# First query chunk interleaved with the input's transposes, small gates unit moved to the value chunks

## The reference, cut to what matters

```python
h = rms_norm(x, norm_g)
proj = jnp.einsum('bsd,dn->bsn', h, w_in)
(q_a, k_a, v_a, o_a, i_a, f_a, z_a, c_q, c_kv, k_r, z_b, g_a, g_b) = jnp.split(proj, offsets, axis=-1)
qk_a = jax.nn.silu(causal_depthwise_conv(jnp.concatenate([q_a, k_a], axis=-1), conv_w))
...
h_a = mlstm_chunkwise(q, k, v, i_a + gate_bias[:H_A], f_a + gate_bias[H_A:])
```

## Time and profile before

| | |
|---|---|
| median of 3 runs | 2112.98 us (2112.61 to 2113.32) |
| the profiled execution | 2112.74 us |
| its span, first to last instruction | 2110.7 us |
| TensorE busy | 2090.6 us, 99% |
| VectorE busy | 1446.0 us, 69% |
| ScalarE busy | 1088.2 us, 52% |
| mean granted clock of TensorE | 0.999 |

### The profile page before, as it was taken

How to read it: one execution, slowest core, us unless ns; L and a number is a source line. 1 busy time by engine, 2 the same in 40 slices (tenths; PEclk the granted TensorE clock), 3 DMA queues, 4 the chain that set the end, 5 groups by cost and what they waited for, 6 DMA issues and landing times.

```text
span 2110.7 us, 24975 instructions
## 1 busy us (share of the span) xinstructions
PE 2090.6 (99%) x10067; PEld 1754.5 (83%) x10067; DVE 1446.0 (69%) x1868; ACT 1088.2 (52%) x1409; POOL 39.2 (2%) x50
## 2 busy tenths in 40 slices
PE   8999999999999999999999999999999999999998
PEld 6888888888888888888888888888888888888886
DVE  5878788875555776556554455566896896797684
ACT  5545555555444675554445454354544554454453
POOL 0000000000000020000000000000000000000000
PEclk9999999999999999999999999999999999999999
DMA  7455555565465544365745542455555465556562
GB/s 270 181 182 197 200 186 213 182 243 193 172 218 198 189 147 171 125 235 199 294 179 181 191 167 100 160 200 185 196 204 193 168 231 185 185 189 219 182 218 98
DMA packets 56563, 402.60 MB, mean 191 GB/s; under 512 B 6240, under 2 KB 6496, under 8 KB 9216
## 3 DMA queue, kind: packets, MB, share of 16 engines
q1 hardware_dynamic: 53648, 380.67, 50.0%
q0 software_dynamic: 2656, 19.81, 2.4%
q10 hardware_dynamic: 144, 0.52, 0.1%
HBM read 392.59 MB, written 8.39 MB: 190 GB/s over the span
## 4 chain that ended last, share of the span: by engine, by line
PE 96%; ACT 1%; DVE 1%; issue 1%; DMA 0%; SPq 0%; POOLq 0%; POOL 0%; DVEq 0%; ACTq 0%
PE proj L617 15%; PE proj L619 15%; PE proj L618 15%; PE proj L1080 11%; PE proj L1083 6%; PE proj L722 4%; PE proj L723 4%; PE proj L724 4%; PE tbank L724 2%; PE tbank L723 2%; PE tbank L722 2%; PE tbank L576 2%; PE bank_a L722 1%; PE bank_a L724 1%; PE bank_a L723 1%; PE bank_b L724 1%
## 5 line engine op out<-in xcount | busy, mean ns | idle before, releaser
L1726 DVE TENSOR_TENSOR w_lo<-raw,w_hi 128x1024 fp32r<-128x1024 f32 x630 | 748.8, 1199 | 521.1 <-ACT w_hi L1186 513.9
L1186 ACT ACTIVATE w_hi<-raw 128x1024 fp32r<-128x1024 f32 x630 | 652.4, 1041 | 757.2 <-PE proj L619 480.8
L617 PE MATMUL proj<-w_hi,a_both 128*128 128x512 f32 x1280 | 513.3, 401 | 0.0
L619 PE MATMUL proj<-w_hi,a_both 128*128 128x512 f32 x1280 | 499.9, 391 | 0.0
L618 PE MATMUL proj<-w_lo,a_both 128*128 128x512 f32 x1280 | 498.4, 389 | 0.0
L619 PEld LDWEIGHTS proj<-w_hi,a_both 128*128 128x128 f32 x1280 | 240.2, 188 | 51.8
L618 PEld LDWEIGHTS proj<-w_lo,a_both 128*128 128x128 f32 x1280 | 240.7, 188 | 47.8
L617 PEld LDWEIGHTS proj<-w_hi,a_both 128*128 128x128 f32 x1280 | 240.6, 188 | 47.0
L1080 PE MATMUL proj<-a_both,w_hi 128*128 128x512 f32 x672 | 168.4, 392 | 0.3 <-DVE a_both L1772 0.3
L1080 PEld LDWEIGHTS proj<-a_both,w_hi 128*128 128x128 f32 x672 | 121.0, 189 | 22.2 <-DVE a_both L1772 0.5
L1186 ACT ACTIVATE w_hi_deep<-raw 128x1024 fp32r<-128x1024 f32 x84 | 85.7, 1025 | 94.1 <-PE proj L1083 57.6
(11 more groups left out here) (519 smaller groups left out, 3000.9 us busy)
## 6 DMA issues: line engine op xcount, KB each, us to landing
raw<-stream SPq DMA_DIRECT2D x359, 1024.0 KB, 4.8
nat<-x SPq DMA_DIRECT2D x4, 512.0 KB, 8.2
z_store<-z POOLq DMA_DIRECT2D x1, 2048.0 KB, 8.3
ga_store<-z POOLq DMA_DIRECT2D x1, 2048.0 KB, 12.3
gb_store<-z POOLq DMA_DIRECT2D x4, 512.0 KB, 7.2
yb<-z_store POOLq DMA_DIRECT2D x4, 512.0 KB, 10.0
ga<-ga_store POOLq DMA_DIRECT2D x1, 2048.0 KB, 8.0
gb<-gb_store POOLq DMA_DIRECT2D x1, 2048.0 KB, 14.5
```

The costliest lines, as they stand in the source:

```text
L617: nc.tensor.matmul(banks[t][:, :], ah, wh, start=first, stop=False)
L619: last = nc.tensor.matmul(banks[t][:, :], al, wh, start=False, stop=end)
L1186: A(hi_places[s][:, 0:width], src, ACT.Copy).then_inc(w_rounded, 1)
L1726: V.tensor_tensor(lo_places[s][:, 0:width], src, hi_places[s][:, 0:width].bitcast(f32), SUB).then_inc(w_rest, 1)
```

## The change

- SyncE: the identity leaves the queue and is issued by ScalarE. x's first quarter goes first, then the first unit in two halves (the first half with a semaphore of its own, `first_half`), then in turn a quarter of x and a unit; `early` and the rest of the constants follow.
- The stream begins with the query chunks. The small unit stands between the two value chunks that are not paired.
- TensorE turns only quarter 0 of x, then begins the first query chunk; the slots after pieces 0, 2 and 4 turn quarters 1, 2 and 3 (`turn_x`), and each piece j waits for `t_by_dve` of its own group.
- ScalarE and VectorE take, quarter by quarter, two groups of x and two pieces of weights. ScalarE does a warming activation at the start; its square sums stand before and after the split of piece 7.
- The small unit is projected between the value chunks (`project_small`) and copied to a buffer of its own, `small`. `gates_slot` runs in the slots of the second value chunk, its last step in slot 6 instead of 7 (the last Exp stays in slot 7). `angles` moves to slots 0 and 4 of the second query chunk.

```diff
--- before.py
+++ after.py
@@ -193,6 +193,7 @@
         z1 = place("z1", [P, TT, D], f32, 160.25)
         z2 = place("z2", [P, TT, D], f32, 176.25)
         scr = place("scr", [P, D], f32, 160.25)
+        small = place("small", [P, TOK], f32, 170.25)
 
         qn_t = place("qn_t", [P, H_B, TOK], f32, 112)
         kn_t = place("kn_t", [P, H_B, TOK], f32, 128)
@@ -350,6 +351,7 @@
         def sem(name):
             return ctx.enter_context(nc.semaphore(name))
 
+        first_half = sem("first_half")
         raw_landed = [sem(f"raw_landed{i}") for i in range(RING)]
         w_rounded = sem("w_rounded")
         w_rest = sem("w_rest")
@@ -460,16 +462,15 @@
         @block.sync
         def _(sp):
             ident_cols = CONSTS["ident"]
-            sp.dma_start(cst[:, ident_cols], consts_in[:, ident_cols]).then_inc(ident_ready, 16)
             for c in range(4):
-                if c == 2:
-                    sp.dma_start(raw[:, 0, :], stream[0]).then_inc(raw_landed[0], 16)
                 cols = slice(c * CW, (c + 1) * CW)
                 sp.dma_start(nat[:, :, cols], x_v[:, :, cols]).then_inc(x_ready[c], 16)
-            sp.dma_start(raw[:, 1, :], stream[1]).then_inc(raw_landed[1], 16)
+                if c == 0:
+                    sp.dma_start(raw[:, 0, 0:PIECE], stream[0][:, 0:PIECE]).then_inc(first_half, 16)
+                    sp.dma_start(raw[:, 0, PIECE:], stream[0][:, PIECE:]).then_inc(raw_landed[0], 16)
+                else:
+                    sp.dma_start(raw[:, c, :], stream[c]).then_inc(raw_landed[c], 16)
             sp.dma_start(early[:, :], early_in).then_inc(early_ready, 16)
-            for u in range(2, RING):
-                sp.dma_start(raw[:, u, :], stream[u]).then_inc(raw_landed[u], 16)
             sp.dma_start(cst[:, ident_cols.stop:], consts_in[:, ident_cols.stop:]).then_inc(cst_ready, 16)
             for u in range(RING, UNITS):
                 sp.wait_ge(w_rest, FIRST_PIECE[u - RING] + 2)
@@ -651,42 +652,50 @@
 
             pe.sem_inc(w_used, RING)
             pe.wait_ge(ident_ready, 16)
-            for g in range(8):
-                if g % 2 == 0:
-                    pe.wait_ge(x_ready[g // 2], 16)
-                if g >= 6:
-                    pe.wait_ge(t_by_dve, g - 5)
-                for b in range(4):
-                    last = nc.tensor.transpose(x_banks[g][:, b * P:(b + 1) * P], from_nat(nat, g)(b), ident)
-                last.then_inc(t_done, 1)
+            def turn_x(c):
+                pe.wait_ge(x_ready[c], 16)
+                for g in (2 * c, 2 * c + 1):
+                    if g >= 6:
+                        pe.wait_ge(t_by_dve, g - 5)
+                    for b in range(4):
+                        last = nc.tensor.transpose(x_banks[g][:, b * P:(b + 1) * P], from_nat(nat, g)(b), ident)
+                    last.then_inc(t_done, 1)
+
+            turn_x(0)
             readers += [by_dve] * 8
             by_dve.add(8)
             tr.add(8)
 
-
-
-            for j in range(2):
-                pe.wait_ge(t_by_dve, 4 * j + 4)
-                pe.wait_ge(w_rest, piece.at(1))
-                s = piece.n % RING
-                for k in range(8):
-                    kt = 8 * j + k
-                    wh, wl = w_hi[:, s, k * P:(k + 1) * P], w_lo[:, s, k * P:(k + 1) * P]
-                    o = proj[0][:, 0:TOK]
-                    nc.tensor.matmul(o, wh, a_hi[:, kt, :], start=(kt == 0), stop=False)
-                    nc.tensor.matmul(o, wh, a_lo[:, kt, :], start=False, stop=False)
-                    last = nc.tensor.matmul(o, wl, a_hi[:, kt, :], start=False, stop=(kt == KT - 1))
-                last.then_inc(w_used, 1)
-                piece.add()
-            chunk.add()
+            def first_slot(j):
+                if j in (0, 2, 4):
+                    turn_x(j // 2 + 1)
+
+            project(a_hi, a_lo, slot=first_slot, before=lambda j: pe.wait_ge(t_by_dve, j + 1))
+
+            def project_small():
+
+                o = proj[2 * (chunk.n % 2)][:, 0:TOK]
+                wait(pe, proj_read, chunk.at(-1) * 2)
+                for j in range(2):
+                    pe.wait_ge(w_rest, piece.at(1))
+                    s = piece.n % RING
+                    for k in range(8):
+                        kt = 8 * j + k
+                        wh, wl = w_hi[:, s, k * P:(k + 1) * P], w_lo[:, s, k * P:(k + 1) * P]
+                        nc.tensor.matmul(o, wh, a_hi[:, kt, :], start=(kt == 0), stop=False)
+                        nc.tensor.matmul(o, wh, a_lo[:, kt, :], start=False, stop=False)
+                        last = nc.tensor.matmul(o, wl, a_hi[:, kt, :], start=False, stop=(kt == KT - 1))
+                    last.then_inc(w_used, 1)
+                    piece.add()
+                chunk.add()
 
 
             def gates_slot(j):
                 tri, ones = early[:, EARLY["tri"]], early[:, EARLY["ones"]]
                 if j == 0:
-                    pe.wait_ge(proj_read, 2)
+                    pe.wait_ge(proj_read, chunk.at() * 2)
                     for t in range(TT):
-                        last = nc.tensor.transpose(bank_b[:, t * P:(t + 1) * P], stg2[:, 0, t * P:(t + 1) * P], ident)
+                        last = nc.tensor.transpose(bank_b[:, t * P:(t + 1) * P], small[:, t * P:(t + 1) * P], ident)
                     last.then_inc(small_t, 1)
                 if j == 2:
                     pe.wait_ge(lf_ready, 1)
@@ -699,7 +708,7 @@
                     for t in range(TT):
                         last = nc.tensor.transpose(bank_b[0:8, t * P:(t + 1) * P], a_nat[:, t, :], ident)
                     last.then_inc(a_row, 1)
-                if j == 7:
+                if j == 6:
                     pe.wait_ge(m_row, 1)
                     for t in range(TT):
                         last = nc.tensor.transpose(bank_a[:, 16 + 8 * t:24 + 8 * t], m_fin[0:8, t * P:(t + 1) * P],
@@ -713,7 +722,6 @@
                 if j in at:
                     group(from_nat(stg, at.index(j)), by)
 
-            project(a_hi, a_lo, slot=gates_slot)
             for i in range(1, 4):
                 project(a_hi, a_lo, slot=lambda j: stg_slot(j, i, at=(1, 3)))
 
@@ -800,7 +808,8 @@
                 chunk.add(2)
 
             project(a_hi, a_lo, slot=lambda j: stg_slot(j, 4, at=(1, 3)))
-            project(a_hi, a_lo)
+            project_small()
+            project(a_hi, a_lo, slot=gates_slot)
             for p in range(PAIRS_IN):
                 pair_in(p)
 
@@ -1172,7 +1181,11 @@
                     if piece.reg is None and piece.n >= PIECES:
                         return
                     u, at, width, summed = WHERE[piece.n]
-                    if piece.n == FIRST_PIECE[u]:
+                    if piece.n == 0:
+                        act.wait_ge(first_half, 16)
+                    elif piece.n == 1:
+                        act.wait_ge(raw_landed[0], 16)
+                    elif piece.n == FIRST_PIECE[u]:
                         act.wait_ge(raw_landed[u % RING], (u // RING + 1 if piece.reg is None else piece.cycle(2 * RING)) * 16)
                     src = raw[:, u % RING, at:at + width]
                     if summed:
@@ -1227,19 +1240,19 @@
                 sums.add()
 
 
+            act.dma_start(cst[:, CONSTS["ident"]], consts_in[:, CONSTS["ident"]]).then_inc(ident_ready, 16)
+            act.wait_ge(pool_init, 1)
+            A(e_warm[:, :], neg_half[:, 0:1], ACT.Copy)
             act.wait_ge(par_ready, 16)
-            for g in range(8):
-                if g in (4, 6):
-                    split()
-                high(a_hi, 2 * g, "norm_g", 2 * g, x_banks)
+            for c in range(4):
+                for g in (2 * c, 2 * c + 1):
+                    high(a_hi, 2 * g, "norm_g", 2 * g, x_banks)
+                split(2 if c < 3 else 1)
             square_sum(scr[:, :], nat[:, 0, :], ss1[:, 0:1])
-            split(3)
+            split()
             square_sum(scr[:, :], nat[:, 1, :], ss1[:, 1:2])
-            split()
-
-            done.add(2)
-            A(stg2[:, 0, 0:TOK], banks()[0][:, 0:TOK], ACT.Copy).then_inc(proj_read, 2)
-
+            split(RING)
+            done.add(NORM_FULL)
 
             def exp_slot(j):
                 if j == 1:
@@ -1278,8 +1291,9 @@
                 if i in (2, 3) and j == 7:
                     round_x_sums(i - 2)
 
-            for i in range(4):
-                pieces(slot=exp_slot if i == 0 else lambda j: k_slot(j, i))
+            stage(inv1, 1)
+            for i in range(1, 4):
+                pieces(slot=lambda j: k_slot(j, i))
                 stage(inv1, i + 1)
 
             tiles = Tally()
@@ -1342,7 +1356,10 @@
                 chunk.add(2)
 
             for i in range(2):
-                pieces(slot=conv_slot if i == 0 else None)
+                if i:
+                    pieces(2)
+                    A(small[:, :], banks()[0][:, 0:TOK], ACT.Copy).then_inc(proj_read, 2)
+                pieces(slot=conv_slot if i == 0 else exp_slot)
```

(33 more changed lines are left out.)

## The result

The changed kernel takes 2121.37 us (median of 5 runs, 2120.93 to 2121.8) against 2113.04 for the kernel before: 8.3 us slower, ratio 1.0039 (95% interval 1.0028 to 1.005). The forecast was 2117.7 in a range up to 2120.0. The direction was right; 3.7 us were missing. The profiled execution took 2120.93 us.

The account below looks back on a forecast made before the run. The prediction took TensorE's queue, busy 99% of the span, to bound the kernel. It summed 2112.74 us + 1.87 (head) + 3.11 (gates) = 2117.7 us, range 2114.6 to 2120.0.

Parts of the forecast that it names:

- Start of piece 0: Head: first transpose at 5.05, then a ScalarE and VectorE chain; first matmul of piece 0 at 10.3 us.
- five terms of that chain: Head, first transpose to first matmul: 1.15 + 0.84 + 0.84 + 1.05 + 1.23, with small latencies 5.1 us.
- Piece 0 at the low clock: Head: eight matmuls at 0.43, four at 0.227, so the first piece takes 4.5 us instead of 2.72.
- Quarter stalls: Head: TensorE waits 0.85 and restarts slowly by 0.1 at pieces 2, 4 and 6: 3 x 0.95 us.
- Turns, plain pieces and the last two waits: Head: three turns 2.79, pieces 1 to 7 19.04, waits for operands of pieces 7 and 8 0.3 us together.
- Head, forecast loss 1.9: Head with the small unit's 5.76: done at 45.54 against 43.68 before, a loss of 1.9 us.
- Table load before Exp: Gates, slot 1 to 2: Exp now loads a table too, uncovered, so TensorE waits longer: +1.46 us.
- Four terms: Gates in the second value chunk: small unit's copy wait gone -0.80, table load +1.46, m_fin +1.45, m_sum +1.0; together +3.1 us.
- m_fin: Gates: VectorE's result, ready for slot 7, is now needed in slot 6, 2.72 earlier: +1.45 us idle.
- m_sum: Gates: pair 0 waits for a sum behind VectorE's split and first sum of weights: 0.9 and a restart, +1.0 us.
- Angles at no cost: Second query chunk: two sets of VectorE operations, 2.8 and 2.6 us, fit beside the convolution without delaying TensorE.
- Rival 1: Head: the low clock lasts longer, 3.5 us more at half pace: +1.7, 2119.4 us; chance 0.15.

Follow-up runs that it names:

- ident_sp: Changed kernel with the identity back at the head of SyncE's queue and nothing on ScalarE's: 2118.06 us, ratio to the kernel before 1.0028.
- par_sp: Changed kernel with the parameters' transfer in SyncE's queue directly behind x's first quarter: 2119.57 us, ratio to the kernel before 1.0028.
- all_four: Changed kernel with the edits of par_sp, exp_early, split_ahead and gates_slots together: 2110.68 us, ratio to the kernel before 0.999.
- split_ahead: Changed kernel with ScalarE and VectorE splitting three pieces behind x's first quarter instead of two: 2118.25 us, ratio to the kernel before 1.0021.
- plain_head: Changed kernel with the head of the kernel before (all eight groups of x turned first): 2117.30 us, ratio to the kernel before 1.0019.
- exp_early: Changed kernel with a one-column Exp behind the small unit's copy, loading Exp's table before slot 1: 2118.21 us, ratio to the kernel before 1.0026.
- fill_slot2: Changed kernel with 15 unused transposes in TensorE's gates slot 2, ahead of the wait for lf: 2119.45 us, ratio to the kernel before 1.003.
- gates_slots: Changed kernel with VectorE's running maximum in slots 3 and 4 and its last gate step in slot 5: 2118.91 us, ratio to the kernel before 1.0026.
- warm_fill: all_four with 15 unused transposes behind the turn of x's first quarter: 2108.97 us, ratio to the kernel before 0.9982.
- par_first: Changed kernel with the parameters' transfer moved from GpSimd's queue to the head of ScalarE's: 2121.39 us, ratio to the kernel before 1.0041.

## Why the prediction was wrong

Two steps failed: the start of piece 0 left out an operand, 1.8 us, and the sum of the gates left out what the wait in slot 2 does to the clock, 1.7 us. The other terms were off by 0.4 at most each.

- **Start of piece 0, forecast 10.3, measured 12.08: wrong by 1.8.** The step that failed is "From there a chain of two engines leads to piece 0". It began at the drained transposes, and the first operation of `high` also needs the parameters. In the earlier trace rows ScalarE's wait ended at 6.65 by the transposes; the parameters had come before that (issued at 1.25, landed after 4.5), so no wait on them showed. The change sent x first and half units right behind, and put a third queue beside them; the parameters, issued at 1.25 as ever, came 2.4 us later. ident_sp and par_sp show it, and with the parameters in hand the chain is right: in all_four it takes 5.2 us from the first transpose to the first matmul. The prediction's five terms of that chain alone add up to 5.1, so its small latencies, said to be in the 5.1, had no share in it.
- **Piece 0 at the low clock, 4.5: measured 4.9** (the turn behind starts at 16.99). Right in kind; the rise came a little later than the 3.5 us taken from the trace. It has a scatter of its own: in the five traces with this head the piece takes 4.5 to 5.1.
- **Quarter stalls, 3 x 0.95: measured 0.95, 0.92, 0.95.** Right, and split_ahead shows the cause. Turns, plain pieces and the last two waits: within 0.1.
- **Head, forecast loss 1.9:** 41.98 + 5.76 - 43.68 = 4.06, as plain_head has it (4.1). The excess is the first two terms.
- **Table load before Exp, +1.46: right.** The wait on `lf` is 1.70, as forecast. From the split's start (144.67) to Exp it is 2.37 against 0.97, so 1.40. The load took 1.28 and Exp began 1.29 behind its start. The 2.66 us for a switch that the Trainium skill gives (ScalarE: Activation LUTs, What ACT_TABLE_LOAD costs) did not appear.
- **What that wait does to the clock: missing, 1.7.** "Four terms" should have been five. TensorE had no idle time over 0.6 us in this stage before, so no row showed what 1.7 us do. The nearest in that trace is an idle time of 1.35 us ahead of 791.44, behind which the granted clock stays at 1.00. exp_early and fill_slot2 take the fall away, one by removing the load and one by removing only the idleness; both bring back the 1.7.
- **m_fin, +1.45, and m_sum, +1.0:** the idle times are 1.29 and 0.61 (forecast 1.45 and 0.9). Right in kind; why they are shorter was not settled, and it is not the longer stall at slot 2, since exp_early has 1.29 and 0.61 without it. gates_slots shows that the order of slots is the cause of both. Gates together: 8.45 - 4.06 = 4.4 = 3.1 + 1.7 - 0.4.
- **Angles at no cost:** right, no wait of TensorE stands between 42 and 146 us.
- Rival 1 named the clock, but at the head; that its price, 1.7, was met at another place is chance.

What stays open: why the parameters' transfer was delayed as much as it was. ident_sp gives back 1.3 of 2.4 us, par_sp goes around it. Which property of the transfers around it decides it (size of their rows, their order, or the number of queues) was not separated. Nor is it known what decides in which executions a wait of 1.7 us brings the clock down.

## What to carry to other kernels

Before work is moved to the front, list every operand of its first instruction and when each lands; a small transfer that was hidden behind a large one can become the start time. Price a wait that is put into a stream of matmuls not at its length but with the clock's fall behind it: here a table load that added 1.4 us to the chain cost 3.2. Where a wait can't be avoided, TensorE can be kept at work in it, as in fill_slot2 and warm_fill. When a loop of prepare steps runs in order on another engine, split for the next round before waiting for this round's late operand.

## What the runs showed of the hardware

- Small transfers beside a stream of large ones: 64 KB, second on ScalarE's queue, took 7.1 us in par_first, and 3.7 as the first there in the changed kernel; 141 KB on GpSimd's took 6.9, 5.6 and 4.6 us (changed kernel, ident_sp, plain_head), 4.3 as the first on ScalarE's.
- Transposes alone can raise TensorE's clock. In warm_fill nothing but transposes ran when their step went from 0.21 to 0.11 us. The Trainium skill (TensorE: Matmul & The Clock Gate, Part 4: PE-mode transpose) says that a transpose does not count as TensorE being busy in the same way; for these float32 transposes the trace disagrees, with the two steps just given, and the measured gain is 1.7 us.
- A wait of 1.7 us in full work can be followed by 3.4 us at 1.2 GHz (149.69 to 153.10), which costs as much again as the wait. It need not be: in gates_slots' profiled run the pace stayed at 0.23. Filling the wait with useless transposes avoided it in fill_slot2. Waits of 1.3 us for `m_fin` brought no fall in any of the eight traces that have them.
